# A two-block transformer kernel: norms of x taken tile by tile, the overflow flag read ahead of the additions, and a variance part written earlier

## The reference, cut to what matters

```
first block, for each of 2 layers:
    h = rms_norm(x, g1) * (1 + sc1) + sh1
    x = x + gate1 * mixer(h)                 # retention and chunk attention, or stick breaking
    h = rms_norm(x, g2) * (1 + sc2) + sh2
    x = x + gate2 * grouped_moe(h)           # 16 experts in 4 groups, top 2 within the best group
second block, for each of 2 layers:
    x = x + rms_norm(mixer_2(rms_norm(x, g[0])), g[1])
    x = x + rms_norm(cross_attention(rms_norm(x, g[2]), mem_n), g[3])
    x = x + rms_norm(swiglu(rms_norm(x, g[4])), g[5])

rms_norm(x, g) = x * rsqrt(mean(x * x, axis=-1) + 1e-6) * g
```

## Time and profile before

| what | value |
|---|---|
| median of 3 runs | 1916.04 us (1915.75 to 1923.29) |
| profiled execution | 1920.38 us |
| its span, first to last instruction | 1918.6 us |
| TensorE matmuls, busy share | 93% |
| VectorE, ScalarE, busy share | 67%, 56% |
| mean granted TensorE clock | 0.955 |

### The profile page before, as it was taken

How to read it: one execution, slowest core, us unless ns; L and a number is a source line. 1 busy time by engine, 2 the same in 40 slices (tenths; PEclk the granted TensorE clock), 3 DMA queues, 4 the chain that set the end, 5 groups by cost and what they waited for, 6 DMA issues and landing times.

```text
span 1918.6 us, 27034 instructions
## 1 busy us (share of the span) xinstructions
PE 1775.5 (93%) x9505; PEld 1478.1 (77%) x9505; DVE 1278.2 (67%) x2020; ACT 1076.6 (56%) x1653; POOL 13.8 (1%) x29
## 2 busy tenths in 40 slices
PE   5998799999999999999999899888999998889998
PEld 4775478888887866888888788576999876669997
DVE  5685658889886666689889753755544555655454
ACT  2443247878874364578878652555444454554443
POOL 1000000000000000000000000000000000000000
PEclk9897799999999999899999997788999998989999
DMA  9876638999994845499899753022656561215552
GB/s 351 307 248 212 215 123 316 317 358 357 323 355 168 302 132 176 138 347 358 322 356 351 238 183 110 23 88 68 193 179 196 167 205 58 88 45 183 190 180 82
DMA packets 217284, 413.07 MB, mean 215 GB/s; under 512 B 13120, under 2 KB 69488, under 8 KB 216800
## 3 DMA queue, kind: packets, MB, share of 16 engines
q1 hardware_dynamic: 214176, 400.74, 60.6%
q0 software_dynamic: 1904, 8.26, 1.3%
q10 hardware_dynamic: 1120, 2.97, 0.4%
HBM read 410.87 MB, written 1.05 MB: 215 GB/s over the span
## 4 chain that ended last, share of the span: by engine, by line
PE 79%; DVE 11%; ACT 5%; issue 3%; DMA 2%; DVEq 0%; SPq 0%; ACTq 0%
PE banks L735 21%; PE banks L737 21%; PE banks L736 21%; DVE weights_low L2090 3%; PE banks L1145 1%; DMA weight_ring<-in_ada_w 1%; DVE row_gains L2361 1%; PE banks L752 1%; PE banks L765 1%; PE banks L999 1%; ACT scratch L1687 1%; PE banks L1000 1%; PE banks L888 1%; PE banks L792 1%; ACT weights_high L1536 1%
## 5 line engine op out<-in xcount | busy, mean ns | idle before, releaser
L2090 DVE TENSOR_TENSOR weights_low<-weight_ring,weights_high 128x1024 fp32r<-128x1024 f32 (+1 forms) x656 | 771.9, 1219 | 181.7 <-ACT weights_high L1536 109.2
L735 PE MATMUL banks<-weights_high,features_parts 128*128 128x512 f32 (+1 forms) x1488 | 593.7, 399 | 22.5 <-DVE features_parts L2523 8.3
L736 PE MATMUL banks<-weights_low,features_parts 128*128 128x512 f32 (+1 forms) x1488 | 583.0, 392 | 0.0
L737 PE MATMUL banks<-weights_high,features_parts 128*128 128x512 f32 (+1 forms) x1488 | 582.7, 392 | 0.0
L1819 ACT ACTIVATE weights_high<-weight_ring 128x1024 fp32r<-128x1024 f32 x384 | 392.2, 1056 | 101.8 <-PE banks L737 73.2
L735 PEld LDWEIGHTS banks<-weights_high,features_parts 128*128 128x128 f32 x1488 | 282.8, 190 | 88.0 <-issue 15.7
L737 PEld LDWEIGHTS banks<-weights_high,features_parts 128*128 128x128 f32 x1488 | 282.1, 190 | 60.1
L736 PEld LDWEIGHTS banks<-weights_low,features_parts 128*128 128x128 f32 x1488 | 282.8, 190 | 55.9 <-issue 1.0
L1536 ACT ACTIVATE weights_high<-weight_ring 128x1024 fp32r<-128x1024 f32 (+1 forms) x176 | 176.1, 1043 | 141.6 <-PE banks L737 90.4
L735 PE MATMUL banks<-features_parts,weights_high 128*128 128x256 f32 x736 | 210.3, 286 | 1.6 <-DVE features_parts L2185 1.5
L737 PE MATMUL banks<-features_parts,weights_low 128*128 128x256 f32 x736 | 208.2, 283 | 0.0
(11 more groups left out here) (385 smaller groups left out, 1705.5 us busy)
## 6 DMA issues: line engine op xcount, KB each, us to landing
weight_ring<-in_exp_w_gate SPq DMA_DIRECT2D x128, 512.0 KB, 5.1
weight_ring<-in_exp_w_up SPq DMA_DIRECT2D x128, 512.0 KB, 5.0
weight_ring<-in_exp_w_down SPq DMA_DIRECT2D x128, 512.0 KB, 5.3
weight_ring<-in_ada_w SPq DMA_DIRECT2D x96, 512.0 KB, 5.5
weight_ring<-in_ffn_wg SPq DMA_DIRECT2D x44, 512.0 KB, 4.3
weight_ring<-in_ffn_wu SPq DMA_DIRECT2D x44, 512.0 KB, 4.6
weight_ring<-in_ffn_wd SPq DMA_DIRECT2D x44, 512.0 KB, 4.2
weight_ring<-in_even_w_in SPq DMA_DIRECT2D x28, 512.0 KB, 5.7
```

The costliest lines, as they stand in the source:

```text
L735: eng.matmul(dst, lh, rh, start=first, stop=False, **kw)
L736: eng.matmul(dst, lh, rl, start=False, stop=False, **kw)
L737: mm = eng.matmul(dst, ll, rh, start=False, stop=last, **kw)
L2090: V(half_of(low(s), i, size), half_of(slot(n), i, size), half_of(high(s), i, size).bitcast(F32), ALU.subtract)\
```

## The change

Four edits, all on ScalarE and VectorE. First, `norm_x` of the first block's layers goes tile by tile on both engines: ScalarE waits for its own square and takes the root of one column behind each tile's square, and VectorE takes the reciprocal of one column and scales that tile before it waits for the next root. Second, VectorE's load of the flag stands ahead of `add_scattered`; the branch stays behind it. Third, in `add_normed`, at the last chunk and where a joint follows (`new`), VectorE waits for the square of the new first tile's first half and writes that tile's part, ahead of the second tile's additions; `norm_new_x` keeps only the second tile's part, behind the first tile's diagonal. Fourth, the norm of the input keeps its old form, so its call names `normalise` itself.

```diff
@@ ScalarE, norm_x(n)
                     square(NB[:, tb, :], X[:, tb, :], tb)
-                eng.wait_ge(squares, sq[0])
-                take_root(SS, TB, D)
+                    if n:
+                        eng.wait_ge(squares, sq[0])
+                        eng.activation(ROOT[:, tb:tb + 1], SS[:, tb:tb + 1], ACT.Sqrt, scale=1.0 / D, bias=EPS_[:, :])\
+                           .then_inc(root_ready, 1)
+                if not n:
+                    eng.wait_ge(squares, sq[0])
+                    take_root(SS, TB, D)
@@ VectorE
             def norm_x():
-                normalise(lambda tb: X[:, tb, :])
+                sqn[0] += TB
+                for tb in range(TB):
+                    roots[0] += 1
+                    eng.wait_ge(root_ready, roots[0])
+                    eng.reciprocal(RSD[:, tb:tb + 1], ROOT[:, tb:tb + 1]).then_inc(*vec.up())
+                    settle()
+                    ins = eng.tensor_scalar(NB[:, tb, :], X[:, tb, :], RSD[:, tb:tb + 1], None, ALU.mult)
+                ins.then_inc(normed, 1)
...
-            def add_normed(gain, places, done):
+            def add_normed(gain, places, done, new=True):
...
                         root_taken(tb)
+                        if i == 3 and new:
+                            eng.wait_ge(squares, sqn[0] + 1)
+                            part_of(4, 2)
                         eng.wait_ge(taken, done - 3 + i)
...
             def norm_new_x():
-                for tb in range(TB):
-                    sqn[0] += 1
-                    eng.wait_ge(squares, sqn[0])
-                    part_of(4 + tb, 2 + tb)
-                    sqn[0] += 1
-                    diagonal(tb)
+                sqn[0] += 2
+                diagonal(0)
+                sqn[0] += 1
+                eng.wait_ge(squares, sqn[0])
+                part_of(5, 3)
+                sqn[0] += 1
+                diagonal(1)
...
+                over = eng.value_load(FLAG[0:1, 0:1], min_val=0, max_val=1)
                 add_scattered(moe, l, 4 * l)
-                over = eng.value_load(FLAG[0:1, 0:1], min_val=0, max_val=1)
                 with eng.If(over == 1):
...
-            norm_x()
+            normalise(lambda tb: X[:, tb, :])
...
-                add_normed(2, [(4 + i, i % 2, i // 2) for i in range(4)], chunks[st[f"cao{l}"][1][-1]]["done"] + 4)
+                add_normed(2, [(4 + i, i % 2, i // 2) for i in range(4)], chunks[st[f"cao{l}"][1][-1]]["done"] + 4, l == 0)
```

## The result

The changed kernel took 1904.7 us (median of 6 runs, 1902.35 to 1908.33) against 1917.7 us of the kernel before (6 runs, 1915.75 to 1923.29) on the same chip: ratio 0.9929, 95% interval 0.9914 to 0.9943, or 13.0 us off. The profiled execution took 1908.33 us (before 1920.38).

A forecast was written before the change was run, and what follows sets the result against it. The prediction saw long TensorE product stages joined by serial stretches where TensorE waits for a norm of x. Gains of 1.5 + 1.7 + 3.3 = 6.5 us off the 1916.04 median gave 1909.5 us, range 1904.8 to 1914.3.

The forecast's parts named there:

- Flag: Behind the last addition of x at both MoE ends: loading the flag ahead of the additions saves 1.5 us.
- I take the load without the gap: At both MoE ends: count 0.89 + 0.62 us of load as saved, while the second joint's 0.40 us issue gap stays.
- the upper bound (1.91): At both MoE ends: the 0.40 us issue gap goes with the load, 0.89 + 1.02 = 1.91 us.
- The load's cover: Ahead of the additions: the moved load falls into VectorE's 1.29 us wait for the first scatter product.
- Norms tile by tile: Norms ahead of MoE 0, odd_in and MoE 1: the first tile's steps fall into waits, saving 1.7 us.
- The middle one: Norm ahead of odd_in: one scaling of 0.67 us goes, the root comes 0.33 us later, saving 0.34 us.
- Variance part: Five second-block joints: first tile's part ahead of the additions saves 3.3 us (three at 0.68, od_out 0.8, ev_out 0.5).
- the prediction's parenthesis: At ev_out: 0.8 us saved instead of 0.5 if TensorE's clock is up.
- none of the joints' VectorE and ScalarE durations depends on what differs there, so I take the sum off the median: Whole kernel: 6.5 us come off the shown median of 1916.04, giving 1909.5 us.
- the median is probably already without that stretch: Argument against a clock gain: the median probably already lacks the long 1.2 GHz stretch, 4.45 us, seen in MoE 1.
- clock, for the better: Shorter idle times keep TensorE at 2.4 GHz; one long stretch of 4.45 us gone gives 1905.1 us; chance 0.14.
- ten terms: The gains at two flag joints, three tile-by-tile norms and five variance-part joints, summing to 6.5 us.

The follow-up runs named there:

- pure shifts: Kernel before with filling matmuls inside product stages: 0.9 us each in even_out and odd_in, ratio 1.0009; in another kernel, 2.3 us in od_in, ratio 1.0022.

## Why the prediction was right or wrong

**Flag: mechanism right, size off.** 0.89 + 1.03 = 1.92 us against 1.5. The failing step is "I take the load without the gap": the first joint's load had no gap in it, and I concluded that the gap would stay. It went, and the upper bound (1.91) was the value. The Trainium skill (Runtime: NRT & Kernel Launch, Instruction fetch mechanics) says that a taken branch out of the fetched window stalls. What stayed behind the branch, 0.58 and 0.19 us, agrees with it, though no trace shows what VectorE's sequencer does in these gaps; nothing in it said that a gap ahead of the branch belongs to it, which was my reading. The load's cover was wrong as well, without cost: it runs beside the splits, not in the wait for the first product.

**Norms tile by tile: right.** 0.67, 0.35 and 0.66 us, sum 1.7 as forecast. The middle one, priced from norm_whole_x's own order, was the least sure (forecast 0.34).

**Variance part: right, 3.4 against 3.3.** Behind cao0, ffn 0 and cao1 it gave 0.6 and not 0.68: the second half's additions began 0.47 us behind the reciprocal (1315.11 - 1314.64), not 0.38, because the part starts 0.11 us after the square sum that it waits for has ended (1314.93 to 1315.04), a step that I had at nothing. The line of that sum in the changed kernel:

```profile
1314.75 0.18 ACT L1600 ACTIVATION_READ_ACCUMULATOR projected<-x_state 128x1 f32 x1
```

Behind ev_out the joint gave 0.80 and not 0.5, for the clock was up there, as the prediction's parenthesis allowed.

**The total: wrong.** The step that failed is in the sum: "none of the joints' VectorE and ScalarE durations depends on what differs there, so I take the sum off the median", with the clock left as it was, and in the rival "the median is probably already without that stretch". The joints gave 7.0 and the rest, 4.5 us over all 12 runs and 6.0 in the first comparison, is TensorE's clock. The stretch in MoE 1 is in typical executions of the kernel before: the unchanged copy has it too. The profiled execution standing 4.3 us over the median proved little: over 17 to 29 runs the medians of the kernel before were 1917.4 to 1918.2, so 1916.04, of three runs, was low. So the rival "clock, for the better" had the mechanism and the direction, and its chance of 0.14 was too small. That its 1905.1 lies 0.4 us from the first median is in part luck: it named one long stretch gone, 4.45 us, but MoE 1's stage became only 2.8 us shorter and MoE 0's longer, and the clock's 4.5 to 6 us are the sum of gains and losses in many stages. Nor was the direction pure chance: each edit alone gained more than its joints by the medians (3.9, 1.2 and 3.9 us; for the norms the interval holds no gain at all), and fills alone gained 4.5 to 7.3 us, while pure shifts gained nothing in total and the changed kernel with its idle times made long again kept little more than its joints. The prediction's last sentence, that a total moving by over 4 us against the sum while the joints show it would be the clock, named the case.

The Trainium skill (TensorE: Matmul & The Clock Gate, Part 1) says that the same program differs from run to run, since the gate's watching isn't tied to the kernel's start. The traces agree in part: MoE 0's stage took 22.00 and 23.59 us in two executions of one kernel. But MoE 1's took 26.45 twice. I took that page's rule as a reason to leave the clock out of the forecast; measured, it is a reason to widen it.

**What stays open.** What makes a given stretch fall to 1.2 GHz was separated for two: at od_in's transposes it is the place, behind the norm ahead of od_in the length of the idle time. For the others, MoE 0 and MoE 1 above all, the two weren't separated: a kernel that shortens the idle times and puts the same time back as work elsewhere, joint by joint, wasn't tried. The clock's parts of the three edits don't add up (9.0 us of excess alone, 3.0 to 6.0 together). And the first 260 us, which no edit touches, took 252.7 to 261.5 us in the traces, which blurs any single profile by more than the sum forecast. So a gain of the clock in one trace, ahead of the first edit above all, is no gain of the edits.

## What to carry to other kernels

Price the joints from rows, as here: ten terms came within 0.5 us of their sum. Then add a term of its own for the granted clock wherever TensorE waits again and again: read the stages behind each wait in more than one execution, and widen the range by a stretch on either side, for a change of a microsecond in a joint can be worth several in stages that it doesn't touch. Before an edit that shortens such waits, try longer fills: in this kernel six to nine more matmuls ahead of three norms gave 7.3 us.

## What was not expected of the hardware

- Filling matmuls that end inside an idle time, and so change no joint, changed the total by 7.3 us (0.9964 [0.9951, 0.9978]) in the first block and by nothing from norm_whole_x on (1.0008 [0.9995, 1.0022]).
- The same 1.08 us idle time in front of the same six transposes went once with 1.37 us and once with 0.88 us, decided by 2.3 us of work put in far ahead of it. The window around them took 17.3 to 17.4 us in all eight traces without that work and without the variance edit, and 15.75 with it.
- At nearly the same moment, 1.04 us of idle time ahead of a norm's transposes left the granted clock at 1.00 and 1.72 us took it to 0.74 over the same six microseconds behind, in one trace each.
- Loading the flag into a register held VectorE's queue 0.89 us at the first joint and 1.02 us with its gap at the second, and costs nothing where it runs beside splits; branching on it is 0.06 us, plus 0.58 and 0.19 us behind it.
